# Four groups of gathered value rows summed on TensorE instead of VectorE, and forgetting scores issued in pairs

## The reference, cut to what matters

```
h   = x + W_out [ forgetting attention (8 heads) || differential attention (4 heads) ]( W_in RMSNorm(x) )
h   = h + PEER( RMSNorm(h) )
out = RMSNorm(h)
```

```
hid = gelu(einsum('thkd,td->thk', u_tab[eidx], xn)) * softmax(top_s)
out = einsum('thk,thkd->td', hid, v_tab[eidx])
```

## Time and profile before

| | |
|---|---|
| time, median of 3 runs | 1541.17 us (1539.67 to 1543.49) |
| the profiled execution: its time | 1541.62 us |
| the profiled execution: its span, first to last instruction | 1539.8 us |
| granted TensorE clock, mean over the span | 0.939 of full |
| busy over the span | PE 1269.3, DVE 1077.6, POOL 751.5, ACT 459.8 us |
| moved by DMA | 596.50 MB, mean 387 GB/s |
| steps 0, 13, 16, 19, 22 begin (DVE's first dot of the step) at | 110.1, 295.3, 334.0, 381.1, 425.3 us |
| step 27 begins; the last hosted row is added | 490.5; 529.7 us |

### The profile page before, as it was taken

The page is one execution under the profiler, slowest core; times in us unless marked ns, Lnnn a source line. Parts: engine busy times, 40 slices in busy tenths (PEclk is TensorE's granted clock), DMA queues, the critical chain, the costliest instruction groups (busy, mean ns, idle before and its releaser), DMA issues.

```text
span 1539.8 us, 13062 instructions
## 1 busy us (share of the span) xinstructions
PE 1269.3 (82%) x3727; PEld 658.2 (43%) x3727; DVE 1077.6 (70%) x2520; ACT 459.8 (30%) x1200; POOL 751.5 (49%) x637
## 2 busy tenths in 40 slices
PE   9999999988888488999787777677886787777778
PEld 7766655665545234444333333233332233332333
DVE  3247699999988867566666676666666766666654
ACT  3432355466343022222222222221222222222212
POOL 0016477675667443454544554445444554444440
PEclk9999999999989699999899999989999999999998
DMA  9669799997999999999999999999999999999995
GB/s 382 250 250 413 275 330 351 370 376 268 340 371 392 391 421 416 421 421 421 421 422 422 421 422 421 421 422 421 422 421 421 422 422 421 422 420 422 421 421 208
DMA packets 99741, 596.50 MB, mean 387 GB/s; under 512 B 11480, under 2 KB 11480, under 8 KB 42328
## 3 DMA queue, kind: packets, MB, share of 16 engines
q0 software_dynamic: 89856, 536.91, 86.0%
q1 hardware_dynamic: 9816, 58.77, 9.6%
HBM read 593.54 MB, written 2.10 MB: 387 GB/s over the span
## 4 chain that ended last, share of the span: by engine, by line
DMA 42%; PE 15%; DVE 6%; POOL 3%; issue 2%; ACT 2%; DVEq 0%; POOLq 0%
PE acc L994 13%; DMA map_mem<-in_peer_uv_dram,eidx 10%; DMA w_ring<-in_peer_uv_dram,eidx 9%; DMA v_all<-in_peer_uv_dram,eidx 7%; DMA act_mem<-in_peer_uv_dram,eidx 6%; DMA v_ring<-in_peer_uv_dram,eidx 3%; DMA mix_mem<-in_peer_uv_dram,eidx 3%; DMA u_ring<-in_peer_uv_dram,eidx 3%; DMA v_ring<-in_peer_v_dram,eidx 2%; PE mm L786 1%; ACT diag L1228 1%; DVE map_mem L1549 1%; DVE w_ring L1549 1%; PE sc L786 1%; POOL v_ring L692 1%
## 5 line engine op out<-in xcount | busy, mean ns | idle before, releaser
L1220 ACT ACTIVATE gel<-hid 128x4 f32<-128x4 f32 x126 | 25.8, 205 | 722.2 <-DVE hid L1549 712.5
L685 POOL DMA_INDIRECT u_ring<-in_peer_u_dram,eidx x112 | 136.8, 1221 | 172.9 <-DVE eidx L1529 99.5
L994 PE MATMUL acc<-v_all,diag 128*128 128x512 f32 x256 | 129.2, 651 | 61.1 <-ACT diag L1228 60.6
L692 POOL DMA_INDIRECT v_ring<-in_peer_v_dram,eidx x112 | 133.4, 1192 | 66.4 <-DVE h L1577 38.0
L1577 DVE SCALAR_TENSOR_TENSOR h<-v_ring,coef,h 128x1024 f32<-128x1024 f32 x112 | 143.9, 1284 | 14.3 <-DMA v_ring<-in_peer_v_dram,eidx 11.3
L994 PE MATMUL acc<-map_mem,diag 128*128 128x512 f32 x248 | 123.3, 644 | 32.0 <-ACT diag L1228 32.0
L994 PE MATMUL acc<-v_ring,diag 128*128 128x512 f32 x248 | 120.1, 629 | 32.3 <-ACT diag L1228 28.7
L1541 DVE CUSTOM_DVE_ANT_0 u_ring<-u_ring,hn 128x1024 f32<-128x1024 f32 x112 | 136.6, 1220 | 14.2 <-DMA u_ring<-in_peer_u_dram,eidx 14.0
L994 PE MATMUL acc<-u_ring,diag 128*128 128x512 f32 x248 | 119.1, 626 | 27.4 <-ACT diag L1228 25.8
L1228 ACT ACTIVATE diag<-ident,coef 128x128 f32<-128x128 f32 x392 | 126.3, 390 | 39.1 <-DVE coef L1567 30.8
L711 POOL DMA_INDIRECT v_all<-in_peer_uv_dram,eidx x64 | 76.1, 1189 | 92.3 <-PE acc L994 81.7
(11 more groups left out here) (281 smaller groups left out, 2331.9 us busy)
## 6 DMA issues: line engine op xcount, KB each, us to landing
w_ring<-in_slabs_dram SPq DMA_DIRECT2D x29, 1024.0 KB, 8.4
v_ring<-in_slabs_dram SPq DMA_DIRECT2D x6, 1024.0 KB, 11.2
u_ring<-in_slabs_dram SPq DMA_DIRECT2D x6, 1024.0 KB, 10.9
map_mem<-in_slabs_dram SPq DMA_DIRECT2D x6, 1024.0 KB, 7.9
h<-in_x_dram SPq DMA_DIRECT2D x4, 512.0 KB, 12.5
u_ring<-in_peer_u_dram,eidx POOLq DMA_INDIRECT x112, 6.9
v_ring<-in_peer_v_dram,eidx POOLq DMA_INDIRECT x112, 7.1
v_all<-in_x_cols_dram SPq DMA_DIRECT2D x3, 512.0 KB, 7.4
```

Source lines behind the costliest of these rows:

```text
L685: nc.gpsimd.indirect_dma_start(out=u_ring[:, c % U_RING, :], out_offset=None, in_=peer_u[0], in_offset=bass.IndirectOffsetOnAxis(ap=eidx[n ...
L692: nc.gpsimd.indirect_dma_start(out=v_ring[:, c % V_RING, :], out_offset=None, in_=peer_v[0], in_offset=bass.IndirectOffsetOnAxis(ap=eidx[n ...
L994: last = nc.tensor.matmul(acc[half][:, :], diag[:, c % COLS, :], v_row(n, c)[:, half * BANK:(half + 1) * BANK], start=first, stop=(n % PH ...
L1220: nc.scalar.activation(gel[:, par, g0:g0 + COLS], hid[:, par, g0:g0 + COLS], ACT.Gelu).then_inc(gelu_done, 1)
```

## The change: what it does

1. `SUMMED = (11, 14, 17, 20)`: the value rows of these four groups of tile 0 are no longer added by DVE. ACT makes a diagonal matrix of each row's coefficients (`sum_diag`, 4 per group, in a new tile `gate_mem` that it shares with the forget gates' scratch), TensorE multiplies each with the gathered row into two product banks (4 rows x 2 halves = 8 products a group, "sum"), and DVE adds the two banks to `h` (`add_sum`, two instructions).
2. Where they stand: the diagonals in gap 2 and the sum in gap 6 of step k + 2 (steps 13, 16, 19, 22); DVE makes the coefficients already in gap 7 of step k + 1; it adds the sum in gap 1 of step k + 3, or before an output product that comes earlier.
3. The ring place of a row counts as free when TensorE has used it (`row_taken`): TensorE's products step `added` for rows 0 to 2 of the group and `mm_full` for the last.
4. Each sum takes a share of 10 in the planner, so the total grows from 551.2 to 591.2 and every other piece moves: to earlier gaps at the front, and away from the sums' steps.
5. Forgetting scores of heads 2i and 2i + 1 are issued together in the even step: both query-key products, then both forget-term products. The odd step issues none.

```diff
@@ -59,6 +59,8 @@
 LATE_HEADS = 4
 LATE_EVERY = 5
 BEHIND = 2
+SUMMED = (11, 14, 17, 20)
+SHARE_SUM = 10.0
 
 
 FOX = 512
@@ -267,8 +269,18 @@
 
     AFTER = [[] for _ in range(SLOTS * GAPS)]
     total, at = sum(share(p) for p in later), 0.0
+    total += SHARE_SUM * len(SUMMED)
+    summed_at = {}
+    for k in SUMMED:
+        summed_at[(k + BEHIND) * GAPS + 2] = ("diagonals", k)
+        summed_at[(k + BEHIND) * GAPS + 2 * COLS - 2] = ("sum", k)
     for p in later:
         k = int(at / total * (SLOTS - 1) * GAPS)
+        while summed_at and k >= min(summed_at):
+            slot = min(summed_at)
+            AFTER[slot].append(summed_at.pop(slot))
+            at += SHARE_SUM if AFTER[slot][-1][0] == "sum" else 0.0
+            k = int(at / total * (SLOTS - 1) * GAPS)
 
         searched = p[2] + p[1] * PH if p[0] == "keys" and (p[1] == 0 or p[2] == 0) else None
         assert searched is None or k < (searched - 1) * GRP * GAPS + 2 * COLS, p
@@ -301,6 +313,8 @@
             MM.append(p)
             if p == ("forget", 0):
                 MM.append(("fturn", 0))
+        elif kind == "sum":
+            MM += [(*p, half) for half in range(2)]
         elif kind == "turn":
             MM.append(p)
         elif kind == "project":
@@ -589,6 +606,12 @@
         def by_row(n, c):
 
             return GRP * n + GRP - 2 + c - (GRP - 2) * COLS + 1
+
+        def row_taken(i):
+
+            if i // COLS in SUMMED and i % COLS == COLS - 1:
+                return mm_full, mm_done(("sum", i // COLS, 1))
+            return added, i + 1 - sum(COLS * k + COLS - 1 <= i for k in SUMMED)
 
         def group_at(k):
 
@@ -836,6 +859,20 @@
                     for c in range(KC):
                         last = nc.tensor.matmul(bk[0:FH, 0:n], wf[:, c, :], actT[:, c, 0:n], start=(c == 0), stop=(c == KC - 1))
                     last.then_inc(mm_full, 1)
+                elif kind == "sum":
+                    k, = p
+                    pe.wait_ge(*row_taken(COLS * k - 1))
+                    banks = [mm_bank((kind, k, half)) for half in range(2)]
+                    for c in range(COLS):
+                        pe.wait_ge(v_in[c % V_RING], 16 * (k * COLS // V_RING + 1))
+                        pe.wait_ge(sum_diag_done, COLS * SUMMED.index(k) + c + 1)
+                        for half in range(2):
+                            last = nc.tensor.matmul(banks[half][:, :], sum_diag[:, c, :], v_ring[:, c % V_RING, half * BANK:(half + 1) * BANK],
+                                                    start=(c == 0), stop=(c == COLS - 1))
+                            if c == COLS - 1:
+                                last.then_inc(mm_full, 1)
+                        if c < COLS - 1:
+                            last.then_inc(added, 1)
                 elif kind == "lamrow":
 
                     pe.wait_ge(dve_const, 1)
@@ -911,27 +948,36 @@
                     scores(g, half, step)
                 values(g, half, step)
 
+            def pair_scores(g, step):
+
+                t, first = at_step(g, 0, step)
+                nk, j = P * (t + 1), GROUPS[g].index(t)
+                if first == 0:
+                    pe.wait_ge(selq_ready, 2 * (t + 1))
+                both = [(HD * (m % 2), m // 2, map_no[(t, m)]) for m in (first, first + 1)]
+                for lo, ch, k in both:
+                    if k >= len(sc_b):
+                        pe.wait_ge(sc_drained, k + 1 - len(sc_b))
+                    nc.tensor.matmul(sc_b[k % len(sc_b)][:, 0:nk], qT[lo:lo + HD, ch, j * P:(j + 1) * P], kv_t[lo:lo + HD, ch, 0:nk],
+                                     start=True, stop=False)
+                for lo, ch, k in both:
+                    nc.tensor.matmul(sc_b[k % len(sc_b)][:, 0:nk], selq[lo:lo + 40, ch, t % 2, :], caug[lo:lo + 40, 0:nk],
+                                     start=False, stop=True).then_inc(sc_full, 1)
+
             def scores(g, half, step):
-                if at_step(g, half, step):
+                if half == 0:
+                    if step % 2 == 0 and at_step(g, half, step):
+                        pair_scores(g, step)
+                elif at_step(g, half, step):
                     t, it = at_step(g, half, step)
                     nk, j = P * (t + 1), GROUPS[g].index(t)
-                    if it == 0:
-                        pe.wait_ge(selq_ready, 2 * (t + 1))
                     for m in maps_of(it):
                         k = map_no[(t, m)]
                         if k >= len(sc_b):
                             pe.wait_ge(sc_drained, k + 1 - len(sc_b))
-                        bk = sc_b[k % len(sc_b)]
-                        if m < FH:
-                            lo, ch = HD * (m % 2), m // 2
-                        else:
-                            lo, ch = HD * ((m - FH) % 2), KC // 2 + (m - FH) // 2
-                        mo = nc.tensor.matmul(bk[:, 0:nk], qT[lo:lo + HD, ch, j * P:(j + 1) * P], kv_t[lo:lo + HD, ch, 0:nk],
-                                              start=True, stop=(m >= FH))
-                        if m < FH:
-
-                            mo = nc.tensor.matmul(bk[:, 0:nk], selq[lo:lo + 40, m // 2, t % 2, :], caug[lo:lo + 40, 0:nk], start=False, stop=True)
-                        mo.then_inc(sc_full, 1)
+                        lo, ch = HD * ((m - FH) % 2), KC // 2 + (m - FH) // 2
+                        nc.tensor.matmul(sc_b[k % len(sc_b)][:, 0:nk], qT[lo:lo + HD, ch, j * P:(j + 1) * P], kv_t[lo:lo + HD, ch, 0:nk],
+                                         start=True, stop=True).then_inc(sc_full, 1)
 
             def turned_map(g, half, step):
                 if at_step(g, half, step - TURN_LAG):
@@ -1153,6 +1199,14 @@
                         act.wait_ge(rstd2_ready, g + 1)
                         nc.scalar.activation(key_sc[:, PH * t + hd, :], bk[:, 0:2 * K1], ACT.Copy,
                                              scale=rstd2[:, t:t + 1]).then_inc(mm_copied, 1)
+                elif kind == "diagonals":
+                    n, par, g0 = group_at(p[0])
+                    act.wait_ge(coef_done, p[0] + 1)
+                    if p[0] != SUMMED[0]:
+                        act.wait_ge(mm_full, mm_done(("sum", SUMMED[SUMMED.index(p[0]) - 1], 1)))
+                    for c in range(COLS):
+                        nc.scalar.activation(sum_diag[:, c, :], ident[:, :], ACT.Copy,
+                                             scale=coef[:, par, g0 + c:g0 + c + 1]).then_inc(sum_diag_done, 1)
                 elif kind == "lambda":
                     asked[0] += 1
                     given[0] += 1
@@ -1407,6 +1464,8 @@
                                             in1=own.unsqueeze(2).broadcast_to([P, NDH, DH]), op=ALU.mult).then_inc(o_drained, 1)
                 elif kind == "outproj":
                     g, sl, t = p
+                    if sums_due:
+                        add_sum(sums_due.pop())
                     bk = mm_wait((kind, *p))
                     if sl >= N_OUT // 2:
                         dve.wait_ge(*emptied(("outproj", g, sl - N_OUT // 2, t)))
@@ -1571,11 +1630,21 @@
 
                 dve.wait_ge(v_in[c % V_RING], 16 * (TOPK // V_RING) * n + 16 * (c // V_RING + 1))
                 dve.wait_ge(coef_done, GRP * n + c // COLS + 1)
-                if n or c:
-                    dve.wait_ge(added, TOPK * n + c)
+                before = (TOPK * n + c - 1) // COLS
+                if c % COLS == 0 and before in SUMMED:
+                    dve.wait_ge(*emptied(("sum", before, 1)))
+                elif n or c:
+                    dve.wait_ge(*row_taken(TOPK * n + c - 1))
                 ht = h[:, n // PH, :]
                 nc.vector.scalar_tensor_tensor(out=ht, in0=v_ring[:, c % V_RING, :], scalar=coef[:, par, c:c + 1], in1=ht,
                                                op0=ALU.mult, op1=ALU.add).then_inc(added, 1)
+
+            def add_sum(k):
+
+                for half in range(2):
+                    bk = mm_wait(("sum", k, half))
+                    hs = h[:, 0, half * BANK:(half + 1) * BANK]
+                    nc.vector.tensor_tensor(out=hs, in0=bk[:, :], in1=hs, op=ALU.add).then_inc(mm_drained, 1)
 
             def hn_tile(t):
 
@@ -1689,13 +1758,17 @@
                     behind = group_at(k - BEHIND)
                     for gap in range(GAPS):
                         c = gap // 2
+                        if gap == 2 * COLS - 1 and k + 1 - BEHIND in SUMMED:
+                            coefs(*group_at(k + 1 - BEHIND))
+                        if gap == 1 and k - BEHIND - 1 in SUMMED and sums_due:
+                            add_sum(sums_due.pop())
                         if grp == 1:
                             topk_second(n + 1, 1 - par, gap)
                         elif gap == GAPS - 1:
                             next_head(n, par, grp)
                         if gap % 2 == 0 and gap < GAPS - 1:
                             dot(n, par, grp * COLS + c)
```

(2 more changed lines are left out.)

18 lines of the change are left out of this document (12 added, 6 removed).

## The result

The kernel after takes 1552.77 us (median of 4 runs, 1550.07 to 1555.89), the kernel before in the same series 1541.78 us. The ratio is 1.007, interval 1.0046 to 1.0093: 11 us slower, where 1542 and a range up to 1551 were forecast. In what follows "+11.0" is always a median less the median of the kernel before in the same series. The profiled execution of after took 1550.07 us, its span is 1548.2.

The account below looks back on a forecast made before the run. DVE, or a gather floor of some 11 us a step, bounds the hosted part; full DMA engines follow. -3.5 + 2.8 - 1.5 - 1.0 + 4 = +0.8 us, so 1542 us; range 1533 to 1551.

Parts of the forecast that it names:

- adds off DVE: Steps 13 to 23: DVE has 15.1 us less work, most lost under a gather floor; -3.5 us kept.
- pairs: Paired forgetting scores: -1.5 us from DVE's score waits in steps 5 to 14, -1.0 up to step 4.
- sums on PE: Steps 13, 16, 19, 22: in-order sums hold PE, POOL's gathers and DVE's take-in; +4 us, bounds 0 and +16.
- moved pieces: Only the forget gates' move was priced, +2.8 us; moved score maps counted at full price in other, DVE-bound steps.
- the gates: Step 4: a dot, coefficients and an add come behind DVE's wait for PE's gate product; +2.8 us, bounds 0 and +2.8.
- floor of 10 to 12 us a light step: Light steps such as 13, 19, 22: eight POOL gathers take 9.9 to 11.9 us whatever DVE does; 11 taken.
- the prediction's own sign: If light steps last 8 to 9 us, the gather floor was wrong.
- Rival D: Forgetting-score pairs wait for two banks, PE loses its lead, products don't overlap: 1548 us; chance 0.06.
- Rival C: Late sums on PE block POOL's gathers, 3 to 4 us a sum, +8 to +12: 1551 us; chance 0.20.
- E: Step 24: DVE's 4.8 us wait for the gelu goes and does not return: 1537 us; chance 0.13.
- B: DVE's saving gets through, no sum late, gathers 1.24 us each; -8.6 to -11: 1532 us; chance 0.18.
- a wait near 5 us: PE behind a sum's last row: by the rows, the clock halves only when PE's wait nears 5 us.

Follow-up runs that it names:

- rows left out: Kernel before with VectorE adding only 16 of 1024 elements per row in the four groups, the rest omitted: 1539.1 us, -3.2, ratio 0.9975.
- places and pairs: Kernel before with pieces moved as in the change and paired forgetting scores, but no sums on TensorE: 1551.8 us, +10.1, ratio 1.0064.
- places only: Kernel before with pieces moved as in the change, no sums on TensorE, single scores: 1555.3 us, +12.4, ratio 1.0084.
- spread: Kernel before with all pieces moved but eleven, put back from step 15 gap 5 to step 17 gap 2; no sums, single scores: 1549.5 us, +7.4.
- short sums: Kernel after with products of 32 columns instead of 512 for the first three rows of each sum: 1548.4 us, +6.1, ratio 1.0041.
- sums early: Kernel after with each sum's diagonals in its step's first gap and the sum in the second: 1565.5 us, +23.2, ratio 1.0149.
- pairs only: Kernel before with the paired forgetting scores alone, no sums and no moved pieces: 1546.1 us, +3.2, ratio 1.0019.

## Why the prediction was wrong, step by step

The parts are added one after another (places, then pairs, then sums), and each line is what the next part changed, so they must add up to the result. They interact, and in another order they split otherwise: pairs first +3.2, then the sums at the old places +15.5, then the moves -7.7.

| step of the sum | forecast | measured |
|---|---|---|
| adds off DVE | -3.5 | -3.2 (rows left out) |
| pairs | -2.5 | -2.3 (places and pairs, less places only; not clear of noise) |
| sums on PE | +4 | +4.1 (11.0 - 10.1, and the relief of 3.2) |
| moved pieces | +2.8, for the gates | **+12.4** (places only) |
| sum | +0.8 | +11.0 |

**The step that failed is the moved pieces.** The prediction costed one event of the move, the gates, and otherwise said that a moved map costs "full price" in its new step. In the sum that was nothing, since it only lowered what the relief keeps. It never asked what up to nine slots of shift do to the pieces that share PE's three score banks with DVE. By themselves the moves measured +12.4. In order of proof: the crowd in step 15 is worth 5.0 us (spread); the moves ahead of step 13 are worth 6.9 by themselves, of which the trace shows 1.6 up to step 5, 2.9 in steps 5 to 12 and 1.2 in step 15. The two together come near the 12.4. Why the crowd costs time is in part argued: PE's wait of 7.66 us for a bank, DVE's waits behind it and the lower clock all stand in the trace, and only the places were varied. In the other order the same fault shows in another term: without moves the sums cost 15.5 us and not 4, so the prediction was wrong on what room for the sums costs, whichever way it is paid.

**The gates** came as forecast at their place: step 5 began 2.7 us later. At the end they are worth 0.5 to 1 us, within what these runs can tell. The late step did not carry to the end of this kernel, which waits elsewhere anyway.

**The adds off DVE** were sized rightly by luck. The floor of 10 to 12 us a light step is refuted by steps 13 and 22 (8.3 and 9.0 us; step 19, 10.4, is within it); by the prediction's own sign the floor was wrong. Where it gave a bound, a light step is followed by a long one: gathers that are not issued in it are issued in the next. That this debt sets the length of the next step is argued; with the rows left out steps 13 and 14 took 9.6 and 14.0 us with no sum in them, and PE was busy for all of both. The prediction had PE run ahead. It did not count that PE, at 23.59 of 24.3 us in steps 13 and 14, had 0.7 us to give and no more as soon as DVE was relieved. (DVE's nines stand in six slices and not in the seven that the prediction names; nothing rests on it.)

**The pairs** have the forecast size only among moved pieces: alone they cost 3.2, with the sums they are worth 13.3. A term read from DVE's small waits for scores could not show that their worth depends on what else PE has to do. Rival D had the time of the pairs alone (1545 or more) but not the reason: the products of a pair do overlap.

**The sums** cost what was said, 4.1 by difference (that the relief stays 3.2 among moved pieces is argued, not measured) and 4.9 by the short sums. Rival C's mark, over 10 us of POOL's waits for PE, is in the trace with 21.3. But C's number, 1551, was near for another reason: its price of 8 to 12 us on four sums is not there, since the change without sums is already at +10.1: a right number by luck. Where nothing is moved, C's mechanism is real and dear: 7.4 us for one sum, and the gain from pieces out of the way is what the moves pay for. E happened in part (step 24 fell from 17.8 to 14.8 us, a wait of 2.8 us for the gelu came back in step 27) and was outweighed. B is excluded: even free adds give 3.2, not 9 to 11.

**The clock.** After waits of 7 us and more PE was slower in several runs (2.05 us for two products that took 1.02 some 6 us later, in sums early). The rule of the Trainium skill that the prediction weighed, "TensorE: Matmul & The Clock Gate", section "HAM oscillation", agrees with this. That it needs a wait near 5 us, as the prediction read from its rows, did not hold: in after, PE had waited 1.94 us ahead of the values in front of step 19's sum, and that sum's first products took up to 1.91 us instead of 1.02. It cost the sum 1.7 us; those of steps 13, 16 and 22 ran at full clock. What the low clock costs depends on who waits: with the spread it went with the shorter step 15, while in pairs only the slow projection (6.62 us instead of 5.38) stood ahead of a score that DVE waited 3.40 us for. Its share of the loss is not measured.

## What to carry to other kernels

Before giving work from one engine to another, price the relief alone: leave the work out and time it. Here that was 3 us of 15 us of busy time, which no way of doing the work elsewhere could beat. In a schedule that spreads pieces by shares, inserting one piece moves all the others, and the moved ones have to be priced as a part of the change: alone they cost as much as the whole change, and without them the inserted ones cost more. An in-order engine's idle time is worth something only where the new piece stands; moved ahead, it waits for its own operands, with all that is queued behind.

## What the runs showed of the hardware that I had not expected

- A TensorE granted 0.51 of its clock over a step with 3.17 us of work for it did not lengthen that step (16.3 us, against 21.6 at 0.61 with 14.74 us of work).
- Giving TensorE less to do (pairs only) lowered its granted clock over steps 5 to 12 from 0.95 to 0.90, and a projection behind its new waits took 6.62 us instead of 5.38.
- Two products on the two halves of the array start within 0.01 us of each other also when they use only 40 of 64 rows (294.37 and 294.38).
- Removing 14.6 us of busy time from VectorE, which is busy 99% of steps 13 and 14, shortened the kernel by 3.2 us, though none of its waits in before was over 5.4 us in total (190 to 505 us). Small waits of a balanced schedule say nothing of how soon the next ones come.
